# FoX sample attention over a paged cache: suffix sums of the log forgets made once for all pages, picked per unit by 16 narrow matmuls

## The chip, the cores and the metric

One NeuronCore of a Trainium2 chip runs the whole program; the other cores are idle. The metric is device time in microseconds (us) of one execution; the median of several executions is compared. Engines are named as in the profile: PE is TensorE's matmul, PEld its weight load, DVE is VectorE, ACT is ScalarE, POOL is GpSimd, SP is the queue that issues most DMAs.

## The reference, cut to what matters

The program is one layer of a decoder, on a prompt of 1024 rows and on 8 sample sequences of 4 new rows each. The change touches only the attention of the 8 sequences over their past. Each past has 4096 rows, kept in 32 pages of 128 rows; a page table names the pages. A score is a query-key product plus a decay: the sum of the log forgets of all past rows that come after the key's row.

```python
lp = logf_past.astype(jnp.float32)
suffix = lax.cumsum(lp, axis=1, reverse=True) - lp
cn = jnp.cumsum(logf, axis=1)
suf_t = suffix.transpose(0, 2, 1)
s_past = jnp.einsum('bqhd,bkhd->bhqk', q, k_past).astype(jnp.float32) * scale
s_past = s_past + cn_t[..., :, None] + suf_t[..., None, :]
...
p = jax.nn.softmax(jnp.concatenate([s_past, s_new], axis=-1), axis=-1).astype(v.dtype)
```

## The kernel before, in words

`attend_sample` works in 16 units: a unit is half of one sequence's past, 16 pages. Its pages of keys (`k_pg`, 16 pages) and of values (`v_pg`, 16 pages) have one buffer each, and every page is a DMA of 256 KB that SP issues. A unit's pages are taken in four groups of four pages, `pp` = 0 to 3. SP issues in a fixed order, in eights: keys of groups 0 and 1 of a unit, values of groups 0 and 1 of the unit before, keys of groups 2 and 3, values of groups 2 and 3. Before it loads a group of keys it waits until PE has transposed that group of the unit before (`t_full`); before a group of values, until PE has used it (`pv_done`).

For each group, PE transposes the four pages of keys into PSUM banks 0 to 3 (L1133, 16 instructions), DVE and ACT copy two banks each to `kT` (`copy_keys`, L1102), and PE multiplies them with the unit's queries (`scores`, L1156). Rows of PSUM bank 4 or 5 (one bank a half) hold, for four pages side by side, 32 rows of (head, query). Between the transposes of groups 1 and 2 stands `decays`, which starts the accumulation in that bank. Before the change it does so with fp32 matmuls on the unit's staged log forgets:

```python
for j, at in quads:
    nc.tensor.matmul(ps[at, 4 + half, :], later_now[:, half, j, :], g.ones[:], ...)
for pp in range(4):
    for j, at in quads:
        nc.tensor.matmul(ps[at, 4 + half, 0:(pp + 1) * P], lf_now[:, half, 4 * j + pp, :],
                         g.after[:, (3 - pp) * P:4 * P], ...)
```

That is 4 matmuls of 512 columns (L1143) and 16 of 128 to 512 columns (L1147). Each is two PE instructions, as all of this kernel's fp32 matmuls are (transposes are one). POOL's `stage` copies what they need for the next unit: queries (L1068) and, for each of 4 query rows, log forgets and later sums (L1071, L1075).

Ahead of the loop stands a preparation. The log forgets of all pages are gathered (L1037), PE transposes them (L1120), DVE copies them to `lfT` (L1275), sums them in quads (L1278), adds up later quads in a chain of seven (L1283), and makes some constants (L1288 to L1292). PE starts the first unit's key transposes as soon as `lfT` is copied; it does not wait for the chain. DVE's share of `copy_keys` stands behind the chain and the constants in DVE's order. SP has issued the first unit's 16 pages of keys before all this, and goes no further until PE frees their slots.

After the loop, the sequences' own new rows, the merge of the softmax parts and the next stages follow; the change does not touch them.

Of the kernel before, what the change touches and what calls it, by code (L numbers as in the profile page):

```python
# [9 lines left out]
ALU = mybir.AluOpType  # L10
ACT = mybir.ActivationFunctionType
AX = mybir.AxisListType

P = 128
# [3 lines left out]
DEC_B, DEC_S = 8, 4  # L18
# [5 lines left out]
H, HD = 8, 64  # L24
# [3 lines left out]
PAGES = 32  # L28
# [867 lines left out]
def attend_sample(nc, io, g, ps):  # L896
# [7 lines left out]
    UP, QUADS = 16, 4  # L904
    R = H * DEC_S
    KC = DA // P
    UNITS = 2 * DEC_B
    KS = UP

    with ExitStack() as ctx:  # L910
        m = Mem(nc, ctx, "sat")
        table_in_order, table = (m.sb(n, [1, DEC_B * PAGES], I32) for n in ("table_in_order", "table"))
        page_rows = m.sb("page_rows", [P, 2], I32)
        lfT = m.sb("lfT", [P, H, DEC_B * PAGES])
        quad_sum, later = m.sb("quad_sum", [P, H, 2 * UNITS * 2]), m.sb("later", [P, H, 2 * UNITS * 2])
# [3 lines left out]
        lf_now, later_now = m.sb("lf_now", [P, 2, UP, R]), m.sb("later_now", [P, 2, QUADS, R])  # L919
# [30 lines left out]
        lfT_done, lfT_copied = m.sems("lfT_done", 4), m.sem("lfT_copied")  # L950
        qk_done, qk_copied, diag_ready = m.sem("qk_done"), m.sem("qk_copied"), m.sem("diag_ready")
        later_ready, consts = m.sem("later_ready"), m.sem("consts")
        staged = m.sems("staged", 2)
# [24 lines left out]
        with nc.Block() as block:  # L978
# [46 lines left out]
            def _(pool):  # L1025
                link = Chain(pool, pool_own)
# [9 lines left out]
                for a in range(2):  # L1036
# [9 lines left out]
                                             base=0, pattern=[[1, R]], channel_multiplier=-DEC_S))  # L1046
# [5 lines left out]
                                             pattern=[[-DEC_S, DEC_B], [1, NS]], channel_multiplier=0))  # L1052
# [7 lines left out]
                rep = [P, UP, H, DEC_S]  # L1060

                def stage(b, half):


                    pool.wait_ge(s_done[half], START + b)

                    pool.sem_inc(seen, 1)
                    nc.gpsimd.tensor_copy(q_now[:, half], q_diag[:, :, bass.ds(b, 1), :].rearrange("p c a r -> p c (a r)"))\  # L1068
                        .then_inc(staged[half], 1)
                    for q in range(DEC_S):  # L1070
                        nc.gpsimd.tensor_copy(  # L1071
                            lf_now[:, half].rearrange("p n (h q) -> p n h q", q=DEC_S)[:, :, :, q],
                            lfT[:, :, bass.ds(b * PAGES + half * UP, UP)].rearrange("p h n -> p n h"))\
                            .then_inc(staged[half], 1)
                        nc.gpsimd.tensor_copy(  # L1075
                            later_now[:, half].rearrange("p n (h q) -> p n h q", q=DEC_S)[:, :, :, q],
                            later[:, :, bass.ds(8 * b + 4 * half, 4)].rearrange("p h n -> p n h"))\
                            .then_inc(staged[half], 1)
# [27 lines left out]
            def _(pe):  # L1106
# [17 lines left out]
                pe.wait_ge(lfT_copied, 4)  # L1124
                quads = [(j, slice(R * j, R * j + R)) for j in range(QUADS)]
# [11 lines left out]
                def decays(b, half):  # L1137
                    pe.wait_ge(staged[half], 9 * b + 9)

                    pe.wait_ge(exped[half], START + b)  # L1140

                    for j, at in quads:
                        nc.tensor.matmul(ps[at, 4 + half, :], later_now[:, half, j, :], g.ones[:],  # L1143
                                         start=True, stop=False, skip_group_check=True)
                    for pp in range(4):
                        for j, at in quads:
                            nc.tensor.matmul(ps[at, 4 + half, 0:(pp + 1) * P], lf_now[:, half, 4 * j + pp, :],  # L1147
                                             g.after[:, (3 - pp) * P:4 * P], start=False, stop=False,
                                             skip_group_check=True)
# [58 lines left out]
                pe.wait_ge(consts, 7)  # L1208
# [49 lines left out]
            def _(dve):  # L1258
# [6 lines left out]
                dve.wait_ge(consts, 7)  # L1265
# [7 lines left out]
                for b in range(4):  # L1273
                    dve.wait_ge(lfT_done[b], 1)
                    nc.vector.tensor_copy(lfT[:, 4 * (b % 2):4 * (b % 2) + 4, (b // 2) * P:(b // 2 + 1) * P],  # L1275
                                          ps[:, b, :].rearrange("p (h n) -> p h n", h=4)).then_inc(lfT_copied, 1)
                dve.wait_ge(lfT_copied, 4)
                link(nc.vector.tensor_reduce(quad_sum[:], lfT[:].rearrange("p h (c n) -> p h c n", n=4), AX.X, ALU.add))  # L1278

                seqs = "p h (b c) -> p h b c"  # L1280
                la, qs = later[:].rearrange(seqs, c=8), quad_sum[:].rearrange(seqs, c=8)
                for c in range(6, -1, -1):
                    last = nc.vector.tensor_tensor(la[:, :, :, c], la[:, :, :, c + 1], qs[:, :, :, c + 1], ALU.add)  # L1283
                    if c:
                        link(last)
                last.then_inc(later_ready, 1)
# [1126 lines left out]
```

## Time and profile before

| what | value |
|---|---|
| times of three runs | 2099.86, 2105.66, 2107.53 us; median 2105.66 us |
| span of the profiled execution | 2103.6 us; its own time is not listed singly, and the span lies inside the range of the three |
| PE, DVE, ACT, POOL busy over the span | 82%, 35%, 20%, 14% |
| this stage, first page load to last | 650 us to 1012 us of the span |
| bytes moved in the execution | 385.44 MB, mean 183 GB/s |

The span runs from the first to the last instruction of the core. A busy share is a mean over stages with different limits, so the stage that the change touches has to be read by itself. The granted clock of PE is given as a share of 2.4 GHz: 1.00 is 2.4 GHz and 0.50 is 1.2 GHz.

### The profile page before, as it was taken

How to read it: one execution, taken by the hardware profiler on the slowest of the kernel's cores; microseconds unless marked ns; L12 is line 12 of the kernel's file. 1: busy time of each engine (PE TensorE's matmuls, PEld its weight loads, DVE VectorE, ACT ScalarE, POOL GpSimd, SP SyncE). 2: the span in 40 equal slices, each digit the busy share in tenths (PEclk: the TensorE clock that was granted, in tenths of full speed). 3: DMA queues.
4: the chain of work that ended last, by engine and by line, in shares of the span. 5: the costliest groups of instructions: out<-in, count | busy, mean ns of one | idle time of the engine just before them, and what ended most of it. 6: DMA issues, size and time to landing. Idle time of an engine off the chain costs nothing. (4 is left out here: it accounts for less than half of the span.)

```text
span 2103.6 us, 30608 instructions
## 1 busy us (share of the span) xinstructions
PE 1718.4 (82%) x11079; PEld 1064.3 (51%) x11079; DVE 732.0 (35%) x1167; ACT 431.1 (20%) x755; POOL 285.6 (14%) x392
## 2 busy tenths in 40 slices
PE   5999998789886988888599999799448898789920
PEld 3444446444444656555399999644224343344410
DVE  2110119344553433343354554254421111111138
ACT  1000011244432222222043343101101111011113
POOL 0000010100002111110032231022300000000034
PEclk8999999777777999999699999999769989899965
DMA  8323420000005999999354545521059878879944
GB/s 309 116 101 103 162 85 3 1 1 0 0 0 172 385 387 387 387 387 387 109 141 120 143 115 134 191 87 70 26 199 313 280 255 283 290 258 325 306 156 155
DMA packets 276134, 385.44 MB, mean 183 GB/s; under 512 B 18220, under 2 KB 175549, under 8 KB 276054
## 3 DMA queue, kind: packets, MB, share of 16 engines
q1 hardware_dynamic: 262904, 336.85, 47.7%
q0 software_dynamic: 8560, 30.97, 4.3%
q10 hardware_dynamic: 4608, 16.78, 2.0%
q8 instruction: 41, 0.67, 0.1%
q14 instruction: 21, 0.17, 0.0%
HBM read 354.48 MB, written 30.07 MB: 183 GB/s over the span
## 5 line engine op out<-in xcount | busy, mean ns | idle before, releaser
L2097 PE MATMUL ps<-we_w_gu,ex_xT 128*128 128x512 f32 x512 | 256.2, 659 | 57.0 <-DMA we_w_gu<-w_exp_up 55.4
L326 PE MATMUL ps<-w_w,g_arena 128*128 128x512 f32 x512 | 228.4, 605 | 7.6 <-issue 4.0
L2097 PEld LDWEIGHTS ps<-we_w_gu,ex_xT 128*128 128x128 f32 x512 | 106.8, 212 | 202.9 <-issue 200.6
L1503 PE MATMUL ps<-mix_x_hi,mix_w_hi 128*128 128x352 f32 x576 | 188.7, 328 | 18.5 <-DVE mix_x_lo L1467 16.8
L1503 PE MATMUL ps<-mix_x_hi,mix_w_lo 128*128 128x352 f32 x576 | 186.9, 324 | 0.0
L1503 PE MATMUL ps<-mix_x_lo,mix_w_hi 128*128 128x352 f32 x576 | 186.5, 324 | 0.0
L1133 PE MATMUL ps<-g_ident,sat_k_pg 128*128 128x128 f32 x1024 | 129.0, 280 | 42.7 <-DMA sat_k_pg<-cache_k 38.7
L326 PEld LDWEIGHTS ps<-w_w,g_arena 128*128 128x128 f32 x512 | 97.6, 193 | 127.2 <-issue 125.9
L1133 PEld LDWEIGHTS ps<-g_ident,sat_k_pg 128*128 128x128 f32 x1024 | 113.9, 144 | 75.6 <-issue 70.1
L1545 DVE TENSOR_TENSOR mix_w_lo<-mix_w_raw,mix_w_hi 128x1024 fp32r<-128x1024 f32 x73 | 125.9, 1756 | 32.9 <-ACT mix_w_hi L1530 25.0
L1102 ACT COPY sat_kT<-ps 128x512 f32<-128x512 f32 x128 | 73.5, 587 | 249.7 <-PE ps L1133 249.7
L1677 PE MATMUL ps<-mo_w_o,m_mT 128*128 128x512 f32 x256 | 114.6, 603 | 11.2 <-DMA mo_w_o<-w_o 11.2
L1503 PEld LDWEIGHTS ps<-mix_x_hi,mix_w_hi 128*128 128x128 f32 x576 | 109.5, 190 | 20.6 <-DVE mix_x_lo L1467 17.6
L741 PE MATMUL ps<-pat_qkT 66*128 66x512 f32 (+3 forms) x192 | 110.7, 714 | 9.8 <-ACT pat_pr L868 6.4
L1102 DVE COPY sat_kT<-ps 128x512 f32<-128x512 f32 x128 | 87.7, 690 | 86.2 <-PE ps L1133 82.0
L2116 PE MATMUL ps<-we_w_dn,ex_aT 128*128 128x512 f32 x256 | 116.4, 597 | 1.4 <-DVE ex_aT L2159 1.4
L2159 DVE COPY ex_aT<-ps 128x256 f32<-128x256 f32 x32 | 13.6, 425 | 284.0 <-PE ps L2105 284.0
L1503 PEld LDWEIGHTS ps<-mix_x_lo,mix_w_hi 128*128 128x128 f32 x576 | 110.3, 191 | 0.0
L1503 PEld LDWEIGHTS ps<-mix_x_hi,mix_w_lo 128*128 128x128 f32 x576 | 109.4, 190 | 0.0
L1530 ACT CAST mix_w_hi<-mix_w_raw 128x1024 fp32r<-128x1024 f32 x72 | 75.0, 1046 | 113.3 <-PE ps L1503 113.3
L1677 PEld LDWEIGHTS ps<-mo_w_o,m_mT 128*128 128x128 f32 x256 | 48.4, 193 | 67.9 <-issue 56.3
L2184 ACT ACTIVATE ex_gate<-ps 128x256 f32<-128x256 f32 x32 | 12.3, 386 | 292.0 <-PE ps L2097 292.0
(371 smaller groups left out, 2140.7 us busy)
## 6 DMA issues: line engine op xcount, KB each, us to landing
sat_k_pg<-cache_k SPq DMA_DIRECT2D x256, 256.0 KB, 7.9
sat_v_pg<-cache_v SPq DMA_DIRECT2D x256, 256.0 KB, 7.9
we_w_gu<-w_exp_gate SPq DMA_DIRECT2D x32, 1024.0 KB
we_w_gu<-w_exp_up SPq DMA_DIRECT2D x32, 1024.0 KB
we_w_dn<-w_exp_down SPq DMA_DIRECT2D x32, 1024.0 KB, 8.3
mix_w_raw<-w_in SPq DMA_DIRECT2D x49, 512.0 KB
g_arena<-w_ada SPq DMA_DIRECT2D x16, 1024.0 KB
y_rows<-ex_y ACTq DMA_DIRECT2D x32, 512.0 KB, 6.8
```

Source lines behind the costliest of these rows:

```text
L326: last = nc.tensor.matmul(ps[:, b, :], g.hT[:, k, t * P:(t + 1) * P], w[s][:, k, :], start=(k == 0), stop=(k == KD - 1))
L741: last = nc.tensor.matmul(ps[:, 2 * (u % 2) + at // 512, 0:n], qkT[:, hh, 0, i * P:(i + 1) * P], qkT[:, hh, 1, at:at + n], start=True, sto ...
L1102: copy(kT[:, pp % 2, :, j * P:(j + 1) * P], ps[:, j, :].rearrange("p (c k) -> p c k", c=KC))\
L1133: last = nc.tensor.transpose(ps[:, j, c * P:(c + 1) * P], k_pg[:, 4 * pp + j, c * P:(c + 1) * P], g.ident[:])
L1503: last = nc.tensor.matmul(out, w[p][:, at], v[:, x, :], start=(i == 0 and k == 0), stop=(i == len(w_chunks) - 1 and k == 2))
L1530: nc.scalar.copy(w_hi[p][:], w_raw[p][:]).then_inc(hi_done[p], 1)
L1545: nc.vector.tensor_tensor(w_lo[p][:], w_raw[p][:], w_hi[p][:].bitcast(F32), ALU.subtract)\
L1677: last = nc.tensor.matmul(ps[:, 2 * b + half, :], mT[:, k, t * P:(t + 1) * P], w_o[:, k, half * 512:(half + 1) * 512], start=(k == 0), sto ...
L2097: last = nc.tensor.matmul(ps[:, 2 + s, :], xT[s][:, k, :], w_gu[s][:, k, :], start=(k == 0), stop=(k == KD - 1))
L2116: last = nc.tensor.matmul(ps[:, 6 + half, :], aT[s][:, k, :], w_dn[s][:, k, half * 512:(half + 1) * 512], start=(k == 0), stop=(k == KE - 1))
L2159: copy(aT[s][:], ps[:, 4 + s, 0:KE * P].rearrange("p (k n) -> p k n", k=KE)).then_inc(aT_copied[s], 1)
L2184: nc.scalar.activation(gate[s][:], ps[:, 2 + s, 0:DE], ACT.Silu).then_inc(gated[s], 1)
```

## The change

Ahead of the loop, four steps take the place of the quad sums and their chain. For each of the 16 units, whose 16 pages times 8 heads fill 128 columns, one matmul with a single column of ones makes each page's total (`page_sums`). One matmul of 128 columns with a triangular matrix makes the suffix sums inside each page (`in_page`). Two small matmuls with masks made by POOL (`later_page`, `same_head`) turn the totals into the sums over later pages (`later_done`). DVE adds these to the suffixes, a unit at a time, and leaves `suffix` with one row for each (head, page) of a unit (`later_ready`). PE waits for all 16 additions before its first key transposes. `lfT` now lies in the second half of `kT`.

In the loop, POOL stages one copy of 128 columns beside the queries. `decays` is 16 matmuls of 128 columns, each with a 0/1 matrix `pick` as its weights, which picks a page's row out of the unit's 128.

```diff
-        quad_sum, later = m.sb("quad_sum", [P, H, 2 * UNITS * 2]), m.sb("later", [P, H, 2 * UNITS * 2])
+        total_lf, later = m.sb("total_lf", [P, 2, DEC_B]), m.sb("later", [P, 2, DEC_B])
+        suffix = m.sb("suffix", [P, UNITS, P])
...
+        lfT = kT[:, 1].rearrange("p c n -> p (c n)").rearrange("p (u m) -> p u m", u=UNITS)
...
 @block.gpsimd
-                nc.gpsimd.memset(later[:], 0.0).then_inc(consts, 1)
+                for dst, compare, step in ((same_head, ALU.is_ge, 0), (later_page, ALU.is_gt, -1)):
+                    link(nc.gpsimd.affine_select(out=dst[:].rearrange(block, h=H), ...))
+                    nc.gpsimd.affine_select(out=dst[:].rearrange(block, h=H), ...).then_inc(picks, 1)
+                link(nc.gpsimd.memset(pick[:], 0.0))
+                nc.gpsimd.affine_select(out=pick[:].rearrange("p n (h q) -> p n h q", q=DEC_S), ...)\
+                    .then_inc(picks, 1)
                 pool.wait_ge(diag_ready, 2 * KC)
-                pool.wait_ge(later_ready, 1)
-                pool.wait_ge(lfT_copied, 4)
+                pool.wait_ge(later_ready, UNITS)
...
-                    for q in range(DEC_S):
-                        nc.gpsimd.tensor_copy(lf_now[:, half]..., lfT[:, :, ...]).then_inc(staged[half], 1)
-                        nc.gpsimd.tensor_copy(later_now[:, half]..., later[:, :, ...]).then_inc(staged[half], 1)
+                    nc.gpsimd.tensor_copy(suffix_now[:, half], suffix[:, bass.ds(2 * b + half, 1), :]
+                                          .rearrange("p a k -> p (a k)")).then_inc(staged[half], 1)
...
 @block.tensor
                 pe.wait_ge(lfT_copied, 4)
+                pe.wait_ge(picks, 3)
+                for u in range(UNITS):
+                    last = nc.tensor.matmul(ps[:, 4, u:u + 1], lfT[:, u, :], g.ones[:, 0:1], start=True, stop=True)
+                last.then_inc(page_sums, 1)
+                for u in range(UNITS):
+                    nc.tensor.matmul(ps[:, u // 4, (u % 4) * P:(u % 4 + 1) * P], lfT[:, u, :],
+                                     g.after[:, 3 * P:4 * P], start=True, stop=True).then_inc(in_page, 1)
+                pe.wait_ge(total_copied, 1)
+                nc.tensor.matmul(ps[:, 5, 0:UNITS], later_page[:], total_lf[:]..., start=True, stop=False, ...)
+                nc.tensor.matmul(ps[:, 5, 0:DEC_B], same_head[:], total_lf[:, 1, :], ...).then_inc(later_done, 1)
+                pe.wait_ge(later_ready, UNITS)
...
 def decays(b, half):
-                    for j, at in quads:
-                        nc.tensor.matmul(ps[at, 4 + half, :], later_now[:, half, j, :], g.ones[:], ...)
                     for pp in range(4):
                         for j, at in quads:
-                            nc.tensor.matmul(ps[at, 4 + half, 0:(pp + 1) * P], lf_now[:, half, 4 * j + pp, :],
-                                             g.after[:, (3 - pp) * P:4 * P], start=False, ...)
+                            nc.tensor.matmul(ps[at, 4 + half, pp * P:(pp + 1) * P], pick[:, 4 * j + pp, :],
+                                             suffix_now[:, half, :], start=(pp == 0), ...)
...
 @block.vector
-                dve.wait_ge(lfT_copied, 4)
-                link(nc.vector.tensor_reduce(quad_sum[:], lfT[:]..., AX.X, ALU.add))
-                for c in range(6, -1, -1):
-                    last = nc.vector.tensor_tensor(la[:, :, :, c], la[:, :, :, c + 1], qs[:, :, :, c + 1], ALU.add)
+                dve.wait_ge(page_sums, 1)
+                nc.vector.tensor_copy(total_lf[:], ps[:, 4, 0:UNITS]...).then_inc(total_copied, 1)
+                dve.wait_ge(later_done, 1)
+                link(nc.vector.tensor_copy(later[:], ps[:, 5, 0:UNITS]...))
+                dve.wait_ge(in_page, UNITS)
+                for u in range(UNITS):
+                    nc.vector.tensor_scalar(suffix[:, u, :], ps[:, u // 4, (u % 4) * P:(u % 4 + 1) * P],
+                                            later[:, u % 2, u // 2:u // 2 + 1], None, ALU.add).then_inc(later_ready, 1)
```

## Rows read from the trace of the kernel before

**Rows 1.** The page's slices: GB/s in 40 equal slices of the span.
```profile
GB/s 309 116 101 103 162 85 3 1 1 0 0 0 172 385 387 387 387 387 387 109 141 120 143 115 134 191 87 70 26 199 313 280 255 283 290 258 325 306 156 155
```

**Rows 2.** Windows: PE, PEld, DVE, ACT, POOL busy (count), PE clock, DMA share, GB/s.
```profile
670.00:680.00 10.00, 10.00 (x128) 7.50 (x132) 3.18 (x5) 2.28 (x4) 2.67 (x11) 0.83 0.61 196
...
780.00:800.00 20.00, 17.11 (x253) 11.29 (x246) 7.21 (x11) 4.46 (x9) 2.72 (x11) 1.00 1.05 387
```

**Rows 3.** The page's DMA issues, keys (values: the same): count, size, us to landing.
```profile
sat_k_pg<-cache_k SPq DMA_DIRECT2D x256, 256.0 KB, 7.9
```

**Rows 4.** Waits from 640 to 1012 us: total, times, longest.
```profile
PE ps L1133 <- DMA sat_k_pg<-cache_k: 38.7, 27, 1.5
```

**Rows 5.** Waits of the SP queue from 674 to 1000 us, all of them.
```profile
SPq L996 <- PE ps L1178: 4.0, 1, 4.0
```

**Rows 6.** Timeline of one unit's `decays`: start us, us, instruction, count, idle before.
```profile
793.43 1.06 PE L1143 MATMUL ps<-g_ones,sat_later_now 128*32 128x512 f32 x8
...
794.32 2.34 PE L1147 MATMUL ps<-g_after,sat_lf_now 128*32 128x128 f32 x32
...
796.47 1.06 PE L1156 MATMUL ps<-sat_kT,sat_q_now 128*32 128x128 f32 x32
...
797.46 0.66 PE L1167 MATMUL ps<-g_ident,sat_pr 128*128 128x128 f32 x4
```

**Rows 7.** Timeline of the preparation and the first unit.
```profile
650.35 25.67 SPq L996 DMA_DIRECT2D sat_k_pg<-cache_k  x24
...
657.05 0.52 POOL L1056 MEMSET sat_later<- 128x512 f32 x1
...
663.15 3.66 PE L1133 MATMUL ps<-g_ident,sat_k_pg 128*128 128x128 f32 x16 [0.78 <-DVE sat_lfT L1275]
...
667.51 0.15 DVE L1288 TENSOR_SCALAR sat_row_mod<-sat_row 128x1 int32<-128x1 int32 x1
...
669.13 1.29 DVE L1102 COPY sat_kT<-ps 128x512 f32<-128x512 f32 x2
...
669.96 3.56 PE L1133 MATMUL ps<-g_ident,sat_k_pg 128*128 128x128 f32 x16 [3.15 <-DVE sat_kT L1102]
...
676.89 4.42 SPq L996 DMA_DIRECT2D sat_v_pg<-cache_v  x8
...
677.47 1.97 PE L1133 MATMUL ps<-g_ident,sat_k_pg 128*128 128x128 f32 x16
```

**Rows 8.** Windows of 1 us, first unit and stream's end, columns as in rows 2.
```profile
670.00:671.00 1.00, 1.00 (x6) 1.00 (x7) 0.42 (x1) 0.00 (x0) 1.00 (x5) 0.54 0.92 291
...
672.00:673.00 1.00, 1.00 (x7) 1.00 (x6) 0.29 (x1) 0.50 (x1) 0.67 (x3) 0.50 0.01 4
673.00:674.00 1.00, 1.00 (x11) 0.36 (x13) 0.40 (x1) 0.44 (x1) 0.00 (x0) 0.75 0.00 0
...
1012.00:1013.00 1.00, 0.77 (x8) 0.00 (x0) 0.00 (x0) 0.00 (x0) 0.00 (x0) 1.00 0.11 41
```

**Rows 9.** Narrow matmuls with 128 columns of weights, of the routing: timeline, then windows.
```profile
1538.83 4.02 PE L1899 MATMUL ps<-rt_token_in_tile,rt_at_row 128*128 128x32 f32 x18 [14.18 <-DVE rt_token_in_tile L1986]
...
1540.00:1541.00 1.00, 1.00 (x7) 1.00 (x6) 0.00 (x0) 0.00 (x0) 0.00 (x0) 0.50 1.08 347
```

**Rows 10.** Matmuls of 128 by 128 by 128 columns of the gating branch: timeline, windows.
```profile
352.44 1.95 PE L513 MATMUL ps<-gm_wsT,z_z 128*128 128x128 f32 x16
...
353.00:354.00 1.00, 1.00 (x11) 1.00 (x10) 0.97 (x2) 0.11 (x1) 0.00 (x0) 1.00 0.00 0
```

**Rows 11.** Groups by form, DVE and POOL: busy us, mean ns of one.
```profile
L1102 DVE COPY sat_kT<-ps 128x512 f32<-128x512 f32 x128 | 87.7, 690 | 86.2 <-PE ps L1133 82.0 <-DVE sat_o_head L1312 0.2
...
L247 DVE TENSOR_SCALAR g_arena<-ps,mod_modT 128x512 f32<-128x512 f32 x8 | 6.5, 810 | 3.7 <-PE ps L214 3.4
...
L1263 DVE COPY sat_kT_new<-ps 128x128 f32<-128x128 f32 x1 | 0.3, 281 | 0.0
...
L156 POOL TENSOR_SCALAR_AFFINE_SELECT g_before<-g_ones 128x128 f32<-128x128 f32 x1 | 0.3, 285 | 0.0
```

More of the change, by code:

```diff
@@ L913, in attend_sample @@
         page_rows = m.sb("page_rows", [P, 2], I32)
-        lfT = m.sb("lfT", [P, H, DEC_B * PAGES])
-        quad_sum, later = m.sb("quad_sum", [P, H, 2 * UNITS * 2]), m.sb("later", [P, H, 2 * UNITS * 2])
+        total_lf, later = m.sb("total_lf", [P, 2, DEC_B]), m.sb("later", [P, 2, DEC_B])
+        suffix = m.sb("suffix", [P, UNITS, P])
+        same_head, later_page, pick = m.sb("same_head", [P, P]), m.sb("later_page", [P, P]), m.sb("pick", [P, UP, R])
         qT, kT_new = m.sb("qT", [P, KC, NS]), m.sb("kT_new", [P, KC, NS])
@@ L952, in attend_sample @@
         later_ready, consts = m.sem("later_ready"), m.sem("consts")
+        in_page, page_sums, later_done, total_copied = (m.sem(n) for n in ("in_page", "page_sums", "later_done", "total_copied"))
+        picks = m.sem("picks")
         staged = m.sems("staged", 2)
@@ L1069, in stage @@
                         .then_inc(staged[half], 1)
-                    for q in range(DEC_S):
[L1071 to L1078, printed above, removed]
+                    nc.gpsimd.tensor_copy(suffix_now[:, half], suffix[:, bass.ds(2 * b + half, 1), :]
+                                          .rearrange("p a k -> p (a k)")).then_inc(staged[half], 1)
                 def keep(b, half):
@@ L1124, in _ @@
                 pe.wait_ge(lfT_copied, 4)
+                pe.wait_ge(picks, 3)
+                for u in range(UNITS):
+                    last = nc.tensor.matmul(ps[:, 4, u:u + 1], lfT[:, u, :], g.ones[:, 0:1], start=True,
+                                            stop=True)
+                last.then_inc(page_sums, 1)
[3 more added lines that the diff above has]
+                pe.wait_ge(total_copied, 1)
+                nc.tensor.matmul(ps[:, 5, 0:UNITS], later_page[:], total_lf[:].rearrange("p a b -> p (a b)"), start=True,
+                                 stop=False, skip_group_check=True)
+                nc.tensor.matmul(ps[:, 5, 0:DEC_B], same_head[:], total_lf[:, 1, :], start=False, stop=True,
+                                 skip_group_check=True).then_inc(later_done, 1)
+                pe.wait_ge(later_ready, UNITS)
                 quads = [(j, slice(R * j, R * j + R)) for j in range(QUADS)]
@@ L1137, in decays @@
                 def decays(b, half):
-                    pe.wait_ge(staged[half], 9 * b + 9)
+                    pe.wait_ge(staged[half], 2 * b + 2)
                     pe.wait_ge(exped[half], START + b)
-                    for j, at in quads:
-                        nc.tensor.matmul(ps[at, 4 + half, :], later_now[:, half, j, :], g.ones[:],
-                                         start=True, stop=False, skip_group_check=True)
                     for pp in range(4):
                         for j, at in quads:
-                            nc.tensor.matmul(ps[at, 4 + half, 0:(pp + 1) * P], lf_now[:, half, 4 * j + pp, :],
-                                             g.after[:, (3 - pp) * P:4 * P], start=False, stop=False,
-                                             skip_group_check=True)
+                            nc.tensor.matmul(ps[at, 4 + half, pp * P:(pp + 1) * P], pick[:, 4 * j + pp, :],
+                                             suffix_now[:, half, :], start=(pp == 0), stop=False, skip_group_check=True)
                 def scores(b, half, pp):
@@ L1207, in _ @@
                     pe.wait_ge(o_read[half], START + DEC_B)
[L1208 removed]
+                pe.wait_ge(consts, 6)
                 for b in range(DEC_B):
@@ L1264, in _ @@
                 dve.wait_ge(qk_copied, 2)
-                dve.wait_ge(consts, 7)
+                dve.wait_ge(consts, 6)
                 for c in range(KC):
@@ L1274, in _ @@
                     dve.wait_ge(lfT_done[b], 1)
-                    nc.vector.tensor_copy(lfT[:, 4 * (b % 2):4 * (b % 2) + 4, (b // 2) * P:(b // 2 + 1) * P],
-                                          ps[:, b, :].rearrange("p (h n) -> p h n", h=4)).then_inc(lfT_copied, 1)
-                dve.wait_ge(lfT_copied, 4)
-                link(nc.vector.tensor_reduce(quad_sum[:], lfT[:].rearrange("p h (c n) -> p h c n", n=4), AX.X, ALU.add))
-                seqs = "p h (b c) -> p h b c"
-                la, qs = later[:].rearrange(seqs, c=8), quad_sum[:].rearrange(seqs, c=8)
-                for c in range(6, -1, -1):
-                    last = nc.vector.tensor_tensor(la[:, :, :, c], la[:, :, :, c + 1], qs[:, :, :, c + 1], ALU.add)
-                    if c:
-                        link(last)
-                last.then_inc(later_ready, 1)
+                    at = slice(4 * (b % 2) * UP, (4 * (b % 2) + 4) * UP)
+                    nc.vector.tensor_copy(lfT[:, 8 * (b // 2):8 * (b // 2) + 8, at].rearrange("p u (h n) -> p h u n", n=UP),
+                                          ps[:, b, :].rearrange("p (h u n) -> p h u n", h=4, n=UP)).then_inc(lfT_copied, 1)
+                dve.wait_ge(page_sums, 1)
+                nc.vector.tensor_copy(total_lf[:], ps[:, 4, 0:UNITS].rearrange("p (b a) -> p a b", a=2))\
+                    .then_inc(total_copied, 1)
+                dve.wait_ge(later_done, 1)
+                link(nc.vector.tensor_copy(later[:], ps[:, 5, 0:UNITS].rearrange("p (a b) -> p a b", a=2)))
+                dve.wait_ge(in_page, UNITS)
+                for u in range(UNITS):
+                    nc.vector.tensor_scalar(suffix[:, u, :], ps[:, u // 4, (u % 4) * P:(u % 4 + 1) * P],
+                                            later[:, u % 2, u // 2:u // 2 + 1], None, ALU.add).then_inc(later_ready, 1)
                 link(nc.vector.tensor_scalar(row_mod[:], row[:], DEC_S - 1, None, ALU.bitwise_and))
```

13 lines of the change are left out of this document (11 added, 2 removed).

## The prediction

> **What bounds the kernel now.** I read the page's slices first. From about 680 to 1000 us of the span the DMA moves 387 GB/s in slice after slice, more than in any other stretch of the kernel [rows 1]. The windows of that stretch give the other side: in 20 us PE is busy for 17.11, DVE for 7.21, POOL for 2.72 [rows 2]. PE looks nearly full, so the next view is what it waits for: over the stage its key transposes stood 38.7 us for pages of keys still on their way [rows 4]. The SP queue, which would wait for PE if PE freed buffers too late, waited for it once from 674 to 1000 us, for 4.0 us [rows 5]. So inside the loop loads set the pace. The bytes agree: 256 loads of keys and 256 of values of 256 KB [rows 3] are 134.2 MB, and at 387 GB/s they take 347 us, against 362 us from the first load at 650 us [rows 7] to the stream's end at 1012 [rows 8]. The 15 us between these are holes at the start, and there the change puts its work.
>
> The timeline of the start shows how the holes come about [rows 7]. SP issues the first unit's 16 pages at once (650.35), then waits for PE to free key slots. PE transposes the first group from 663.15, right behind the last copy of the log forgets, for 3.66 us. The second group has to wait for DVE, which comes to its key copies only at 669.13, behind the quad chain and the constants; PE transposes it from 669.96 to 673.5. The stream meanwhile runs dry: 4 GB/s in the microsecond at 672, and 196 in the mean of 670 to 680 [rows 2, 8]. After that group SP issues the first values (676.89) and is not held by PE again but for the 4.0 us above. What happens to the end of the second group happens to the whole load stream, and through it to the end of the stage and of the kernel.
>
> **In the loop: what goes costs nothing, and so gives nothing.** `decays` of one unit takes PE from 793.43 to the first scores at 796.47, 3.04 us [rows 6]. The new one is 16 matmuls of 128 columns on 32 columns of weights, which is the shape and number of one `scores` group, 796.47 to 797.46, so 1.0 us. PE saves 2.0 us in each of 16 units, 32 us in all. It has 20 minus 17.11, 2.9 us of idle in each 20 us already, spent on loads; the saving becomes more of that wait. POOL's staging shrinks too, and POOL is busy for 2.72 of 20 us [rows 2]. Both I cost at nothing. Their cover is the stream of 387 GB/s; if that cover were gone, they would be worth up to the 32 us.
>
> **Ahead of the loop: a chain that PE has to wait for.** Before, PE's first key transposes followed the copies of `lfT` directly, at 663.15 [rows 7]. Now, from that moment:
>
> Page totals: 16 fp32 matmuls of one column with 128 columns of weights, 32 PE instructions. The nearest row is the routing's matmul with the same weights and 32 columns: 18 instructions in 4.02 us, 0.223 each, at a granted clock of 0.50 [rows 9], so 7.1 us. The moving side is so short there that the weight load must be the price. PE is cold here as there: the key transposes at 663.15 take 3.66 us, those at 677.47 only 1.97 [rows 7].
>
> In-page suffixes: 32 instructions of 128 columns. The gating branch did 16 of that form in 1.95 us at clock 1.00, 0.122 each [rows 10]. [...] So 3.5 us at half speed (14 instructions at 0.244) and 18 at 0.122, 2.2 us: 5.7 us.
>
> Sums over later pages: two matmuls, four instructions at 0.122 and the way to DVE, 0.6 us. DVE's copy of `later`, 16 columns, is bounded by 0 and the 0.281 us of a 128-column copy [rows 11]; with the hand-off 0.3 us. The copy of the totals lies beside the in-page matmuls and costs nothing; uncovered it would cost at most that 0.281.
>
> The 16 additions on DVE, 128 columns out of PSUM with one scalar operand a partition: a plain copy of that size takes 0.281 us. What scalar operands add is seen at 512 columns: 0.810 with two of them, 0.690 for a plain copy [rows 11], so 0.12 at most. Between 0.281 and 0.401 I take 0.37, nearer the upper end because most of that extra should be per instruction: 5.9 us.
>
> Sum 7.1 + 5.7 + 0.6 + 0.3 + 5.9 = 19.6 us: PE starts keys at 682.75 instead of 663.15. It has then been idle for six microseconds. An idle gap of three before 669.96 took the clock down to 0.50 [rows 8], so the first group again takes 3.66 us, to 686.4. The five constants now run behind the additions, as long as before (667.51 to 669.13), to 684.4, and DVE has copied its two banks when PE is through with the first group. So the wait of 3.15 us ahead of the second group [rows 7] goes, and the clock is up again some 3.5 us after 682.75: the second group takes about 2.1 us, to 688.5. Before it was through at 673.5. The load stream is late by 15.0 us.
>
> POOL's new masks replace a memset of 0.52 us from 657.05: four selects of 128 columns at 0.285 [rows 11], a memset of 0.52 and a select of four times 0.285 at most make 2.8 us, to 659.9. PE wants them at 663.15, and DVE's queries wait for one step less. No cost; cover is 3.2 us. POOL's first staging waits for the additions and takes two short copies, hidden behind eight groups of transposes and copies. The memory moved (`lfT` into the unused half of `kT`) costs nothing: PE's last read of it is ahead of PE's first key transpose in PE's own order, and the four copies that write it are of the same size.
>
> The four key pages freed first are under way when the second four are freed, and from there SP's order and the rates are those of before, shifted. **In sum** the profiled 2103.6 us become 2118.6; its span lies 2.1 below the median of the runs, and the median becomes 2105.66 + 15.0 = 2120.7 us, 0.7% more. I take half a per cent, 10.5 us, as what a measurement of this kernel can tell from no change: the three runs lie 7.7 us apart.
>
> **Both ends.** Cheapest: everything at clock 1.00, 32 times 0.122 twice (7.8), 0.6, 0.2, and 16 copies at 0.281 (4.5), 13.1 us, then two groups of 1.97: the second through at 680.2, 6.7 late, 2112.4. Dearest: in-page all at half speed (7.8), 1.1 for the two sums, additions at 0.401 (6.4), 22.7 us, then 3.66 and 3.56 us: 693.1, 19.6 late, 2125.3.
>
> **Rivals.** *The loop gives the time back.* If the 387 GB/s were what PE's turns let through, the 32 us would come off the loop: 15.0 - 32 = -17, 2089 us. PE's 17.11 of 20 us [rows 2] speaks for it; its waits for keys, an SP that hardly waits for PE, and a rate that stays on 387 through units of different phase speak against it. It decides from the point where more than 15.0 us come back, that is where 134.2 MB take less than 332 us: a loop above 404 GB/s. The Trainium skill (DMA: Bandwidth & Descriptors, Specifications) puts the fabric's ceiling at 435 GB/s, above the 387 of [rows 1]; by that figure 134.2 MB would take 309 us, an estimate, and the loop could gain up to 38. Chance 0.10, of which 0.02 ends inside half a per cent.
>
> *The preparation is cheaper.* If PE's clock rises early and stays up, page totals and suffixes take 7.8 us instead of 12.8: 3.9 + 3.9 + 0.6 + 0.3 + 5.9 = 14.6, keys from 677.75, a first group of 3.66 (it still follows an idle gap), a second of some 2.3: through at 683.7, 10.2 late, 2115.9, no measurable change. The routing's narrow matmuls held 0.50 in the window shown and in the four others from 1538 to 1543 [rows 9], which speaks against it. The Trainium skill (TensorE: Matmul & The Clock Gate, What's actually happening) says that the throttled state is the default and that activity releases it; if one-column matmuls count as activity it would give this case, and the routing's row does not bear it out. Chance 0.18, with the cases where run spread hides the loss.
>
> *It does not do what it says*: `decays` may not shrink to 1.0 us, if PE is held by something else than columns there. By the first part that would change PE's wait and not the time, so it has no price of its own.
>
> **Numbers.** The forecast has 0.72, its own range 2112 to 2127. Slower by over 0.5%: 0.72. Within 0.5%: 0.18 + 0.02 = 0.20. Faster: 0.08. The range reaches from 2108 to 2127: the two ends, less 4 and plus 2 for the runs' spread (5.8 below the median, 1.9 above); outside are mainly the 0.10 of the loop rival.
>
> **What would show it.** After the first 16 pages the stream stands still from about 667 to 687 us; PE's first key transposes start near 683, behind 16 additions of some 0.37 us; then 387 GB/s again, with PE's busy time down by 1.8 in each 20 us and its wait for keys up by as much; each later stage shifted by 15. Wrong would be: windows in the loop above 395 GB/s or a stage shorter than 362 us, additions below 0.3, or a clock of 1.00 during the page totals.

## The result, and the profile after

The changed kernel takes 2126.14 us (median of 7 runs, 2120.56 to 2128.5); the kernel before took 2105.77 us in the runs beside it. The ratio is 1.0098, 95% interval 1.0078 to 1.0119: slower by 20.4 us (16.4 to 25). The forecast was 2120.7, range 2108 to 2127: the measured time lies 0.9 us below the upper end of the range, and the 15.0 us that were forecast lie below the interval of the difference.

The page's slices of the changed kernel (GB/s in 40 equal slices of the span) have the shape of [rows 1]: the plateau on 387 still stands, only its first slice is lower, 110 instead of 172.

```profile
GB/s 311 111 105 100 158 84 3 1 1 0 0 0 110 378 387 387 387 387 386 137 131 146 119 119 139 143 136 60 45 150 305 264 270 303 275 265 323 322 165 155
```

The timeline of the changed kernel's preparation and first unit (start us, us, instruction, count, idle before and what ended it), which answers to [rows 7]:

```profile
653.08 38.56 SPq L1000 DMA_DIRECT2D sat_k_pg<-cache_k  x24
...
660.33 3.29 DVE L1288 COPY sat_q_diag<-sat_qT 64x32 f32<-64x32 f32 x7 [0.19 <-issue]
...
661.90 1.69 POOL L1069 TENSOR_SCALAR_AFFINE_SELECT sat_pick<-sat_pick 128x512 f32<-128x512 f32 x1
...
663.65 2.48 DVE L1294 COPY sat_kT<-ps 128x512 f32<-128x512 f32 x4
...
666.19 6.99 PE L1135 MATMUL ps<-g_ones,sat_kT 128*128 128x1 f32 x32 [0.86 <-DVE sat_kT L1294]
...
673.04 5.50 PE L1139 MATMUL ps<-g_after,sat_kT 128*128 128x128 f32 x32
...
678.38 0.29 PE L1142 MATMUL ps<-sat_total_lf,sat_later_page 128*128 128x16 f32 x2
...
678.52 0.37 PE L1144 MATMUL ps<-sat_total_lf,sat_same_head 128*128 128x8 f32 x2
...
678.92 0.17 DVE L1300 COPY sat_later<-ps 128x16 f32<-128x16 f32 x1 [5.53 <-PE ps L1144]
679.13 4.22 DVE L1303 TENSOR_SCALAR sat_suffix<-ps,sat_later 128x128 f32<-128x128 f32 x16
...
683.41 5.35 PE L1155 MATMUL ps<-g_ident,sat_k_pg 128*128 128x128 f32 x32 [4.53 <-DVE sat_suffix L1303]
...
692.50 4.60 SPq L1000 DMA_DIRECT2D sat_v_pg<-cache_v  x8
```

Read down PE's rows: page totals, in-page suffixes, two small matmuls, a wait of 4.53 us for the additions on DVE, and only then key transposes, at 683.41. SP's first row is the load stream: the last 8 of its 24 key pages, those of the second unit, are released by those transposes, and the first values follow at 692.50. Start from the first key load, since the stages ahead of it drift by a few us from run to run (650.35 before, 653.08 here, 653.8 in another profile of the kernel before): first keys on PE after 30.3 us instead of 12.8, the first two groups done after 35.7 instead of 23.2.

Windows of the changed kernel (PE, PEld, DVE, ACT, POOL busy with counts, PE's granted clock, DMA share, GB/s), to set beside [rows 2, 8]:

```profile
670.00:680.00 10.00, 8.88 (x51) 8.79 (x51) 1.22 (x6) 0.00 (x0) 0.00 (x0) 0.67 0.01 2
680.00:690.00 10.00, 6.59 (x80) 6.42 (x84) 7.49 (x23) 2.35 (x4) 1.25 (x4) 0.83 0.18 55
690.00:700.00 10.00, 10.00 (x174) 8.71 (x167) 4.56 (x7) 3.53 (x6) 0.00 (x0) 1.00 1.00 344
...
780.00:800.00 20.00, 16.59 (x224) 12.39 (x217) 7.43 (x11) 4.21 (x9) 0.84 (x4) 0.91 1.05 387
...
671.00:672.00 1.00, 1.00 (x7) 1.00 (x6) 0.00 (x0) 0.00 (x0) 0.00 (x0) 0.50 0.00 0
...
684.00:685.00 1.00, 1.00 (x7) 1.00 (x6) 0.93 (x3) 0.00 (x0) 0.84 (x3) 0.50 0.03 8
```

The hole in the stream is there: 2 and 55 GB/s in the 20 us in which PE prepares. Inside the loop 387 GB/s again, as in [rows 2], though PE has less to do. A window of 20 us is shorter than a unit and catches another part of it in each profile (PE's 17.11 is 18.33 in a second profile of the kernel before, the 16.59 is 15.44 in a second one of the changed kernel), so what PE does in the loop is compared over 300 us further down.

The waits of the changed kernel, for keys and of the SP queue (total us, times, longest), beside [rows 4, 5]:

```profile
PE ps L1155 <- DMA sat_k_pg<-cache_k: 47.6, 17, 3.5
...
SPq L1000 <- PE ps L1196: 15.4, 12, 4.4
```

PE waits for keys 8.9 us longer in all, in fewer but longer waits. SP, held by PE once before, is now held 12 times for the release of value pages: not forecast.

I call **stage** the time from the first key load's issue to the start of the last value matmul: 363.2 us before, 377.7 after, so 14.5 more. To the next stage's first matmul it is 15.1 more. What comes after that took 1048.3 us before and 1048.5 after, in this pair of profiles. The rest of the profiled difference of 18.0 us (spans 2103.6 and 2121.6), 2.7, lies ahead of the first load.

### The profile page after: what moved, and what is told of

Same layout as the page of the kernel before. It is cut to its first block and busy times, and to the rows that moved or that the text cites. A ratio compares the mean times of both kernels' runs of the same rounds, so it can differ in the third digit from the quotient of the medians.

```text
span 2121.6 us, 30380 instructions
## 1 busy us (share of the span) xinstructions
PE 1714.0 (81%) x11019; PEld 1087.9 (51%) x11019; DVE 731.6 (34%) x1177; ACT 431.4 (20%) x755; POOL 258.1 (12%) x285
## 5 line engine op out<-in xcount | busy, mean ns | idle before, releaser
L1521 PE MATMUL ps<-mix_x_hi,mix_w_hi 128*128 128x352 f32 x576 | 188.3, 327 | 20.4 <-DVE mix_x_lo L1485 16.7
L1155 PE MATMUL ps<-g_ident,sat_k_pg 128*128 128x128 f32 x1024 | 142.8, 299 | 54.3 <-DMA sat_k_pg<-cache_k 47.6
L1155 PEld LDWEIGHTS ps<-g_ident,sat_k_pg 128*128 128x128 f32 x1024 | 126.5, 154 | 86.8 <-issue 72.4
L1174 PE MATMUL ps<-sat_kT,sat_q_now 128*32 128x128 f32 x2048 | 74.6, 290 | 0.0
```

The source lines that it names most:

```text
L1155: last = nc.tensor.transpose(ps[:, j, c * P:(c + 1) * P], k_pg[:, 4 * pp + j, c * P:(c + 1) * P], g.ident[:])
L1174: last = nc.tensor.matmul(ps[at, 4 + half, pp * P:(pp + 1) * P], q_now[:, half, c, :], kT[:, pp % 2, c, j * P:(j + 1) * P], start=False, s ...
L1521: last = nc.tensor.matmul(out, w[p][:, at], v[:, x, :], start=(i == 0 and k == 0), stop=(i == len(w_chunks) - 1 and k == 2))
```

## The experiments

The theory: PE's new work ahead of the first keys holds up the load stream, by 15 us, and nothing else in the kernel decides. The rivals: the loop gives time back, or costs something of its own. All ratios are to the kernel before, run on the same chip; each stage is read from one profiled execution.

**The two kernels again.** Neither is edited; this is the spread of the stage.

Kernel before:

> The kernel before, unchanged. In the first profiles every kernel but this one had its first key load 1.4 to 3.7 us later in the span, in stages that no edit touches. If that is drift from run to run: first key load between 651 and 654 us here, or the stage of the same length (363 us from the first key load to the last matmul of values, within 1 us) with other stages moved by some us; ratio 1.000 within 0.002. If something in the changed kernels delays the earlier stages: first key load at 650.4 again.

Changed kernel:

> The changed kernel, unchanged. If its loss is the stage's alone: 377 to 379 us from the first key load to the last matmul of values, against 363, and a ratio near 1.007; what goes beyond 15 us is drift of other stages and of the runs. If other stages lose too: ratio 1.009 or more again, with the first key load 2 us or more later than in the copy of the kernel before.

Before: ratio 1.0004 (0.9981 to 1.0026), stage 362.3 us. After: 1.0101 (1.0074 to 1.0128), stage 378.8. So the stage's difference is 14.5 in the first pair and 16.5 in this one; going by these two pairs, a single profile's stage is good to about 1 us. The first key load came at 653.81 before and 652.74 after, so the later start in the first pair was drift. The ratio of the changed kernel, 1.0101, is again above the 1.007 that was expected if the stage alone were longer.

**Preparation alone.** The kernel before, with the new preparation ahead of its first keys; its results go unused, and the old sums and wide matmuls stay.

```diff
                 pe.wait_ge(lfT_copied, 4)
+                for u in range(UNITS):
+                    last = nc.tensor.matmul(ps[:, 4, u:u + 1], lfT[:, ...], g.ones[:, 0:1], ...)
+                for u in range(UNITS):
+                    nc.tensor.matmul(ps[:, u // 4, ...], lfT[:, ...], g.after[:, 3 * P:4 * P], ...)
...
+                pe.wait_ge(added, UNITS)
...
+                for u in range(UNITS):
+                    nc.vector.tensor_scalar(suffix[:, u, :], ps[:, u // 4, ...], rsum_all[:, u:u + 1], ...)
```

> The kernel before, with the changed kernel's preparation added in front of its first key transposes and its loop left as it was (the results of the added work are not used). If the loss sits in the preparation, through the load stream that it holds up: PE's first keys 17 us later after the first load than before, the second key group 12 to 13 us later, the stage 12 to 16 us longer, about 2119 us, a ratio of 1.006 to 1.008. If the changed loop carries a part of the loss (lower PE clock, SP waiting for PE), this kernel loses 3 us or more less than the changed one.

Measured: 1.0089 (1.0058 to 1.0121), stage 376.1 us, 12.9 and 13.8 above the two profiles of before. Timeline of this kernel, then its window and wait inside the loop:

```profile
666.63 6.99 PE L1129 MATMUL ps<-g_ones,sat_lfT 128*128 128x1 f32 x32 [0.78 <-DVE sat_lfT L1290]
...
673.48 5.59 PE L1133 MATMUL ps<-g_after,sat_lfT 128*128 128x128 f32 x32
...
679.67 4.23 DVE L1308 TENSOR_SCALAR sat_kT<-ps,sat_rsum_all 128x128 f32<-128x128 f32 x16
...
683.95 5.38 PE L1148 MATMUL ps<-g_ident,sat_k_pg 128*128 128x128 f32 x32 [4.53 <-DVE sat_kT L1308]
```

```profile
780.00:800.00 20.00, 17.11 (x233) 11.50 (x226) 7.77 (x11) 4.35 (x9) 2.73 (x11) 1.00 1.05 387
```

```profile
PE ps L1148 <- DMA sat_k_pg<-cache_k: 39.2, 28, 1.5
```

Keys begin 30.3 us after the first load and the second group ends at 35.6, the changed kernel's own values, while the loop is that of [rows 2, 4]: the same 17.11 us and 387 GB/s, and 39.2 us of waits for keys beside 38.7. The preparation carries most of the loss: 12.9 to 13.8 us of the 14.5 to 16.5 in the stage.

**Loop alone.** The kernel before with narrow `decays`: the four matmuls of 512 columns and the wide parts are gone, so the sums over later pages are left out of the scores.

```diff
-                    for j, at in quads:
-                        nc.tensor.matmul(ps[at, 4 + half, :], later_now[:, half, j, :], g.ones[:], ...)
                     for pp in range(4):
                         for j, at in quads:
-                            nc.tensor.matmul(ps[at, 4 + half, 0:(pp + 1) * P], lf_now[...],
-                                             g.after[:, (3 - pp) * P:4 * P], start=False, ...)
+                            nc.tensor.matmul(ps[at, 4 + half, pp * P:(pp + 1) * P], lf_now[...],
+                                             g.after[:, 3 * P:4 * P], start=(pp == 0), ...)
```

> The kernel before, with only decays made narrow: 16 matmuls of 128 columns a unit; the sums over later pages are left out of the scores. If loads set the loop's pace: 387 GB/s as before, no change within 3 us, PE's wait for keys up by what it saves or its clock down. If PE's turns had set the pace: up to 32 us faster, 2074 to 2095 us. If the shorter loop harms (clock falls, last group of values used later): 2 to 5 us slower.

Measured: 1.0014 (1.0001 to 1.0027), stage 365.8 us, 2.6 and 3.5 above before (the profiled execution, 2119.2 us, is the longest of this kernel's 13; the median of the 13 is 3.1 us above that of the kernel before). The windows of the loop and of its last unit, the key transposes of that unit, and the waits:

```profile
780.00:800.00 20.00, 16.66 (x260) 12.43 (x260) 7.87 (x12) 5.26 (x10) 2.52 (x11) 1.00 1.05 387
...
1004.00:1006.00 2.00, 2.00 (x19) 1.24 (x12) 0.48 (x1) 0.06 (x1) 0.00 (x0) 1.00 0.53 193
```

```profile
998.49 3.61 PE L1133 MATMUL ps<-g_ident,sat_k_pg 128*128 128x128 f32 x16 [3.18 <-DMA sat_k_pg<-cache_k]
```

```profile
PE ps L1133 <- DMA sat_k_pg<-cache_k: 51.6, 21, 3.7
...
SPq L996 <- PE ps L1175: 15.2, 10, 6.3
```

Less work on PE does not shorten the loop; 387 GB/s stands, and the stage gets, if anything, longer. The last unit shows how. PE waits 3.18 us for keys, its transposes then take 3.61 us instead of 1.97 (granted clock 0.52 from 1000 to 1002), the values are used and freed later, SP waits up to 6.3 us, and the stream falls to 193 GB/s. The signs that the changed kernel has and the preparation alone has not (long key waits, SP held ten times or more, a loop clock of 0.92 in the mean) come from the loop's part. The two parts' ratios add up to 1.0103, beside 1.0098 and 1.0101 for the whole change.

**Totals out of the in-page matmul.** The changed kernel without the one-column matmuls; the in-page one gets a 129th column, of ones, and bank 7 takes the small sums.

```diff
-                    last = nc.tensor.matmul(ps[:, 4, u:u + 1], lfT[:, u, :], g.ones[:, 0:1], ...)
...
-                    nc.tensor.matmul(ps[:, u // 4, ...], lfT[:, u, :], g.after[:, 3 * P:4 * P], ...)
+                    nc.tensor.matmul(ps[:, u // 3, (u % 3) * (P + 1):(u % 3 + 1) * (P + 1)],
+                                     lfT[:, u, :], g.after[:, 3 * P - 1:4 * P], ...)
```

> The changed kernel, with the 16 one-column matmuls taken away: the in-page matmuls take a column of ones along (129 columns) and so give the page totals too. If the preparation's whole chain is on the path of the loads: the 7.0 us of the one-column matmuls go and two small DVE copies come (about 0.5 us), so 6 to 7 us faster than the changed kernel, about 2119 to 2120 us. If the page totals are not on the path, no change.

Measured: 1.0093 (1.0069 to 1.0118), stage 373.4 us. Its timeline:

```profile
666.46 5.56 PE L1135 MATMUL ps<-g_after,sat_kT 128*128 128x129 f32 x32 [0.96 <-DVE sat_kT L1290]
...
673.55 4.23 DVE L1301 TENSOR_SCALAR sat_suffix<-ps,sat_later 128x128 f32<-128x128 f32 x16
...
677.83 6.57 PE L1151 MATMUL ps<-g_ident,sat_k_pg 128*128 128x128 f32 x32 [4.53 <-DVE sat_suffix L1301]
```

Keys come 24.4 us after the first load, 5.9 earlier than in the changed kernel. But the first two groups take 6.57 us instead of 5.35, so the second group is through 31.0 us after the first load, 4.7 earlier, and the stage is 4.3 to 5.4 us shorter. In the time, where 6 to 7 us were expected, no gain shows.

**Values of the first unit into the hole.** Only SP's order changes: the first unit's values are issued before the second unit's keys, on the changed kernel and on the kernel before.

```diff
+                unit(0, 0, None)
+                for first in (0, 2):
+                    values(0, 0, first)
+                unit(0, 1, None)
+                unit(1, 0, (0, 1))
...
```

On the changed kernel:

> The changed kernel, with SP issuing the first unit's 16 pages of values right behind its keys, ahead of the second unit's keys, which wait for PE. PE's work and waits are the same. If the loss is the stream standing still while PE prepares: 4.2 MB, 10.8 us at 387 GB/s, fill the hole, 8 to 11 us faster than the changed kernel, about 2116 us. If the loss is PE's own time ahead of the loop, no change.

On the kernel before:

> The kernel before, with SP issuing the first unit's values ahead of the second unit's keys. Its stream also has holes in the first unit, some 7 us of lost load time. If holes in the stream are what time is lost to: 3 to 6 us faster than before, about 2101 us, stage 357 to 360 us. If not: no change in the stage.

On the changed kernel: 1.0066 (1.0040 to 1.0091), stage 371.3 us, 6.4 and 7.5 less than without, where 8 to 11 were expected. Windows of this kernel:

```profile
670.00:680.00 10.00, 7.61 (x45) 7.52 (x45) 2.50 (x11) 0.00 (x0) 0.00 (x0) 0.73 0.94 344
680.00:690.00 10.00, 7.86 (x102) 7.50 (x103) 6.21 (x18) 2.34 (x4) 1.24 (x4) 0.83 0.28 82
...
700.00:710.00 10.00, 10.00 (x184) 7.83 (x188) 3.65 (x6) 3.14 (x6) 0.83 (x4) 1.00 0.81 285
```

The stretch that had 2 GB/s now has 344. Part of it is lost again at the restart, 285 GB/s from 700 to 710, where only keys are left to load for a while; that they follow PE's pace there is my reading. This is the strongest support for the theory: the PE chain is untouched (first keys 30.4 us and the second group's end 35.7 us after the first load, as without), only bytes have moved into the hole, and the stage gets shorter. On the kernel before the same order takes 1.6 to 2.5 us off the stage (360.7) and nothing off the time, 1.0000 (0.9973 to 1.0027), where 3 to 6 us were expected. Its hole is smaller.

**Both.** The last two edits of the changed kernel together.

> The changed kernel with both mends: page totals out of the 129-column matmuls, and the first unit's values ahead of the second unit's keys. If both gains come out of the same hole and add up (4.3 and 6.4 us of the stage): stage 366 to 369 us, 3 to 6 us longer than before, a ratio of 1.001 to 1.003, about 2109 us. If they overlap: stage about 371 us as with the second mend alone.

Measured: 1.0038 (1.0009 to 1.0067), stage 368.4 us, 9.3 and 10.4 below the changed kernel's. The best variant of the change, still not ahead of the kernel before.

**PE kept busy.** If long idle waits bring PE's clock down and that costs the last microseconds, then useless work should bring them back. The 16 matmuls of `decays` are done three or four times over, starting each bank anew each time.

```diff
-                    for pp in range(4):
+                    for pp in 3 * list(range(4)):
```

The kernels with four times have `4 *` there.

Three times, on the changed kernel:

> The changed kernel, with decays' 16 narrow matmuls issued three times over (each pass overwrites the one before), so that PE is held in the loop about as long a unit as before, 3.0 us; the preparation is the changed one. If the loop's loss is PE's clock, which falls while PE waits over 3 us for keys: clock 1.00 through the loop, longest wait for keys 1.5 to 1.7 us instead of 3.5, the stage 375.5 to 376.5 us like that of the kernel before with the preparation added, 2 us shorter than the changed kernel's 377.7 and 378.8, although PE does more. If work in the loop simply adds to the time: 378 us or more.

Three times, on the variant with both edits:

> The changed kernel with the three mends together: page totals out of the 129-column matmuls, the first unit's values ahead of the second unit's keys, decays' matmuls three times over. If the three losses are separate: stage 366 to 367 us against 368.4 without the third, 3 to 4 us longer than the kernel before, a ratio of 1.001 to 1.003. If the third mend does nothing here: 368 us or more.

Four times, on the changed kernel:

> The changed kernel with decays' 16 matmuls issued four times over, 3.8 us of PE a unit: more than the 3.0 before, while with three times (2.8 us) PE still waited 2.0 us for keys in the last unit and its clock fell there. If the loss at the stream's end comes from the clock that falls during such a wait: clock 1.00 in the last unit, longest wait for keys there under 1.5 us, the last 16 value loads no longer held up, stage 375.5 to 376.5 us. If not: 377.5 to 379 us again, and the loss at the end is something else.

Four times, on the loop alone (sums over later pages left out there too):

> The kernel before with narrow decays (sums over later pages left out of the scores), issued four times over. With one pass the stage was 365.8 us against 363.2 and 362.3. If that loss is the clock in the last unit: 362 to 363.5 us, clock 1.00 there. If the loss belongs to the narrow form itself: 365 us or more.

| kernel | stage us | stage without the repeats | mean granted clock in the loop | PE's wait for keys, us in all and longest |
|---|---|---|---|---|
| changed, three times | 379.0 | 377.7, 378.8 | 0.99 | 42.0, 2.0 |
| both edits, three times | 368.9 | 368.4 | 0.99 | 38.5, 1.8 |
| changed, four times | 378.0 | 377.7, 378.8 | 1.00 | 30.8, 1.5 |
| loop alone, four times | 363.2 | 365.8 | 1.00 | 29.9, 1.5 |

The ratios of the first two are 1.0077 (1.0055 to 1.0098) and 1.0078 (1.0054 to 1.0102); the last two ran once each, 2132.56 and 2102.88 us beside 2102.99 for the kernel before. The changed kernel's ratio is lower with three times (1.0077 beside 1.0098 and 1.0101), but the intervals overlap and the stage is no shorter. The window of the loop alone with four times, then its wait for keys:

```profile
780.00:800.00 20.00, 18.47 (x353) 14.47 (x352) 7.85 (x11) 5.26 (x10) 2.70 (x11) 1.00 1.05 387
```

```profile
PE ps L1133 <- DMA sat_k_pg<-cache_k: 29.9, 26, 1.5
```

Two things follow. With PE busy 18.47 of 20 us the stream still moves 387 GB/s there: PE's load between 16.59 and 18.47 hardly touches the loop's pace (over 300 us it is 387 GB/s in the changed kernel and 385 with four times, about 1.5 us of loads). And the clock does come back with the work, but the stage only in the kernel with the old preparation (365.8 to 363.2, the value of before, one profile each); on the changed kernel and on the variant with both edits it stays where it was. So the clock as the cause of the last 2 us of the whole stage is borne out on one kernel and missed on two; the last unit by itself is taken up below. The time of the second kernel is higher than that of the variant it is built on while the stages agree; outside the stage their two profiles differ by 7.4 us (1057.1 and 1049.7).

## Why the prediction was right, point by point

**What bounds the kernel.** Right. The loop keeps 387 GB/s with 16.59, 16.66, 17.11 and 18.47 us of PE work in 20, and the loop alone is no faster (1.0014), so the rival by which the loop gives the time back is refuted. So is the rival that `decays` might not shrink: from its first matmul to the first scores it takes 0.9 us (688.69 to 689.59 in the first unit) where it took 3.04 [rows 6].

**The preparation holds up the stream.** Right in place: 12.9 to 13.8 us of the stage come with the preparation alone. The size of the whole stage, 14.5 to 16.5 us where 15.0 were forecast, agrees partly by luck, as the next two points show: the second key group was late by 12.5 us and not by 15.0, and a loss in the loop that was put at nothing made up for it. Term by term, in the changed kernel:

| term | forecast us | measured us |
|---|---|---|
| page totals, 32 PE instructions | 7.1 | 6.99 |
| in-page suffixes | 5.7 | 5.50 |
| sums over later pages and the copy of `later` (678.38 to 679.13) | 0.9 | 0.75 |
| 16 additions on DVE | 5.9 | 4.22 |
| first two key groups | 5.75 | 5.35 |

The narrow matmuls did run at a clock of 0.50 (the window at 671), as in [rows 9], and cost the same as there, so the rival of a cheaper preparation falls as well. The Trainium skill (TensorE: Matmul & The Clock Gate, What's actually happening) has activity release the throttle; 6.99 us of one-column matmuls did not release it here. The forecast's 5.7 us for the in-page suffixes has 3.5 us at half speed in it, and no run shows that term by itself: the suffixes took 5.50 us in all, at a granted clock of 0.50 in each microsecond from 673 to 676, 0.71 in the next and 1.00 in the one at 677.

**The step that was mis-sized** is the 16 additions: 5.9 forecast, 4.22 measured. I had 16 times the duration of one, 0.37. The group's row of the changed kernel gives busy us and mean ns of one:

```profile
L1303 DVE TENSOR_SCALAR sat_suffix<-ps,sat_later 128x128 f32<-128x128 f32 x16 | 4.2, 342 | 0.0
```

One takes 342 ns, close to 0.37, but 16 of them take 4.22 us, 264 ns apiece: consecutive ones overlap. By that spacing it is below the 0.3 that the prediction named as a sign of being wrong. Of the 2.5 us by which the second group was less late than forecast, this term is 1.7 and the key groups 0.4; the other terms give the rest.

**The step that failed** is "Both I cost at nothing": PE's saving in the loop was to become more waiting for keys, with PE busy for 1.8 us less in 20, which is 27 or 28 us less in 300. Windows of 300 us from some 50 us after the first key load, of the kernel before (its second profile) and of the changed kernel:

```profile
704.00:1004.00 300.00, 262.19 (x3740) 178.75 (x3736) 118.88 (x168) 73.61 (x140) 35.71 (x145) 1.00 1.05 387
```

```profile
703.00:1003.00 300.00, 253.57 (x3583) 190.92 (x3576) 115.76 (x167) 72.58 (x137) 10.62 (x52) 0.91 1.05 387
```

PE's busy time fell by 8.6 us only (10.2 in the changed kernel's second profile), and its mean clock from 1.00 to 0.91. At full clock 0.91 times 253.57 would be 231 us, an estimate, near the 234 or 235 that were forecast: the work did shrink as forecast, and PE took longer over it. The waits for keys grew by 8.9 us in the first pair of profiles and 11.9 in the second, and got longer singly (3.5 instead of 1.5), SP was held 12 times, and the loop's part by itself made the stage 2.6 to 3.5 us longer. This loss and the 2.5 us forecast too much for the preparation about cancel, which is why the stage agrees with the forecast.

**Where the two losses lie.** The third key group of the last unit is one that PE waits for in every profile, so the start of its transposes dates the stream. In the kernel before and in the changed one:

```profile
994.48 1.97 PE L1133 MATMUL ps<-g_ident,sat_k_pg 128*128 128x128 f32 x16 [1.28 <-DMA sat_k_pg<-cache_k]
```

```profile
1009.21 1.97 PE L1155 MATMUL ps<-g_ident,sat_k_pg 128*128 128x128 f32 x16 [3.37 <-DMA sat_k_pg<-cache_k]
```

| kernel | first key load to that group, us | from there to the last value matmul, us |
|---|---|---|
| before, two profiles | 344.1, 343.1 | 19.1, 19.2 |
| changed, two profiles | 356.1, 356.2 | 21.6, 22.5 |
| preparation alone | 357.0 | 19.1 |
| loop alone | 344.4 | 21.4 |
| totals out of the in-page matmul | 351.4 | 22.0 |
| changed, four times | 357.9 | 20.1 |
| loop alone, four times | 343.9 | 19.3 |

Up to that group the changed kernel is 12.6 us late in the mean, which is the lateness of its second key group (12.5); without the one-column matmuls the two are 7.8 and 7.9. So the preparation's delay is carried through the loop nearly unchanged. The loop's part is lost behind that group, where 4 pages of keys and 24 of values are still to come, 19.0 us at 387 GB/s: 2.4 to 3.4 us in the changed kernel, about 2 in the loop alone, none with the preparation alone. With four times, and a clock of 1.00, it is 0.1 to 0.2 us in the loop alone and about 1 in the changed kernel; but there the group came 1.7 to 1.8 us later than in the changed kernel, so the stage did not get shorter, and no run shows why it came later.

**What stays open.** First, by what chain those last 2 us are lost in the changed kernel. In its second profile the last unit shows the one told above; its transposes, a 2-us window of its stream, and SP's wait:

```profile
1008.97 3.67 PE L1155 MATMUL ps<-g_ident,sat_k_pg 128*128 128x128 f32 x16 [3.57 <-DMA sat_k_pg<-cache_k]
```

```profile
1018.00:1020.00 2.00, 2.00 (x45) 1.23 (x48) 0.30 (x1) 0.58 (x1) 0.00 (x0) 1.00 0.84 218
```

```profile
SPq L1000 <- PE ps L1196: 17.4, 10, 7.1
```

But in the first profile the same transposes took 1.97 us behind a wait of 3.37, with no fall of the clock, and the loss was there too (21.6 us behind that group, beside 19.1). Second, the measured 20.4 us are more than the stage's 14.5 and 16.5. The interval begins at 16.4, so the stage may be all of it. Yet a surplus of this kind shows in nearly every kernel with the new preparation: in the eight sets of several runs that have it, the time lost (the ratio's part of the time before) exceeds the stage's loss by 0 to 10 us, 5 in the mean, an estimate from the figures above, and in the three sets without it by 2 at most. What follows the stage took from 1043.4 to 1058.1 us over the 14 profiles, with no clear order between the four with the old loop (1046.4 to 1054.6) and the ten with a narrow one (1043.4 to 1058.1); whether the change costs anything there was not settled.

## What to carry to other kernels

In this stage, whose loads set the pace, work taken from a waiting engine gave nothing back and even cost 2 to 3 us at the end, and the delay put ahead of the first release of load buffers was paid in full (12.5 us at the second key group, 12.6 at the last unit). So before moving sums out of such a loop, look for the point from which the load stream hangs on that engine, and give the stream buffers to fill, or bytes in another order, across the new work. Price a run of small instructions by their spacing in a row of the trace, not by the duration of one.

## What the runs showed of the hardware that was not expected

- PE's granted clock fell inside the loop when PE got less to do: means of 0.91 to 0.93 with narrow `decays`, 0.99 with three times the narrow matmuls, 1.00 with four times or the old wide ones. In the loop alone a wait of 3.18 us was followed by 16 transposes in 3.61 us, in the changed kernel's first profile one of 3.37 by the same 16 in 1.97. The Trainium skill (TensorE: Matmul & The Clock Gate, HAM oscillation — how this bites in real kernels) describes matmul loops in which waits for loads throttle PE again and again; the means agree with that, the second of these two waits does not.
- 16 consecutive DVE additions out of PSUM, 128 columns each, take 342 ns singly and 264 ns apiece.
- Seven DVE copies of 64 by 32 took 3.29 us while POOL ran its selects, and 1.43 before, when POOL had none there. The log forgets' copies were behind by about 0.3 us for it. That POOL is the cause was not tried by itself.
